# Copying the spare rows of the experts' buffer in 18 parts during the attention steps, on one Trainium2 core

## What is computed

```python
hp = layer_norm(concat([meta, x_prompt]));  hs = layer_norm(x_sample)
q_g, k_g, v_g, r_g, log_a, q_a, k_a, v_a, gate_a, gate_b = split(h @ w_in)
o_g = gated linear attention (4 heads, chunks)      # y_g = rms(o_g) * silu(r_g)
o_a = sliding-window attention (16 heads, window 128, bias, sinks)
h1  = layer_norm(ALPHA * h + (sigmoid(gate_a) * y_g + sigmoid(gate_b) * o_a) @ w_out)
f   = sum over the top 2 of 32 experts of w * (silu(x @ w_gate) * (x @ w_up)) @ w_down
h2  = layer_norm(ALPHA * h1 + f)
```

## Time and profile before

| | us |
|---|---|
| median of 3 runs | 1911.17 (1908.79 to 1911.86) |
| profiled execution, its own time | 1909.03 |
| its span, first to last instruction | 1906.9 |
| TensorE busy | 1734.5 (91%) |
| VectorE busy | 1221.0 (64%) |
| ScalarE busy | 883.9 (46%) |
| GpSimd busy | 306.3 (16%) |
| chain that ended last: TensorE's share | 40% |

### The profile page before, as it was taken

One profiled execution on the slowest core, in us unless ns is written; L12 is line 12 of the kernel. 1 busy time (PEld: TensorE's weight loads), 2 busy tenths in 40 slices (PEclk: granted clock), 3 DMA queues, 4 the chain that ended last, 5 costly groups with the idle time before them and its releaser, 6 DMA issues. The chain is left out here.

```text
span 1906.9 us, 28797 instructions
## 1 busy us (share of the span) xinstructions
PE 1734.5 (91%) x9022; PEld 1463.8 (77%) x9022; DVE 1221.0 (64%) x1695; ACT 883.9 (46%) x1446; POOL 306.3 (16%) x386
## 2 busy tenths in 40 slices
PE   4899999899899999999978899379999999999955
PEld 4889999688788878878846788268888888888832
DVE  6411110577778767777753333868988988988917
ACT  4322221344344434444411122338778778788723
POOL 3200000122412232232210111010000010010025
PEclk9889999899999999999967899579999999999978
DMA  6379521434333333422359424379999999999854
GB/s 207 108 238 289 171 68 52 142 103 144 115 123 125 126 130 103 158 90 89 95 191 321 146 99 185 123 273 397 419 411 414 417 411 409 419 413 408 330 214 194
DMA packets 183312, 422.90 MB, mean 222 GB/s; under 512 B 24976, under 2 KB 123168, under 8 KB 158424
## 3 DMA queue, kind: packets, MB, share of 16 engines
q1 hardware_dynamic: 129776, 321.93, 45.8%
q0 software_dynamic: 20048, 69.06, 10.2%
q10 hardware_dynamic: 33408, 30.94, 4.6%
HBM read 354.83 MB, written 78.55 MB: 227 GB/s over the span
## 5 line engine op out<-in xcount | busy, mean ns | idle before, releaser
L1801 DVE TENSOR_TENSOR wm_lo<-raw,wm_hi 128x2048 fp32r<-128x2048 f32 x192 | 434.3, 2290 | 70.1 <-ACT wm_hi L1297 66.5
L1297 ACT CAST wm_hi<-raw 128x2048 fp32r<-128x2048 f32 x192 | 363.4, 1912 | 72.9 <-PE PS L1934 44.8
L1932 PE MATMUL PS<-w_hi,hT_hl 128*128 128x512 f32 (+1 forms) x584 | 232.9, 399 | 12.0 <-DMA hT_hl<-hl_dram 7.1
L1933 PE MATMUL PS<-w_lo,hT_hl 128*128 128x512 f32 (+1 forms) x584 | 227.0, 389 | 0.0
L1934 PE MATMUL PS<-w_hi,hT_hl 128*128 128x512 f32 (+1 forms) x584 | 226.6, 388 | 0.0
L1932 PE MATMUL PS<-wm_hi,xT_hi 128*128 128x512 f32 x512 | 203.7, 398 | 2.9 <-DVE xT_lo L1863 2.9
L1934 PE MATMUL PS<-wm_hi,xT_lo 128*128 128x512 f32 x512 | 200.8, 392 | 0.0
L1933 PE MATMUL PS<-wm_lo,xT_hi 128*128 128x512 f32 x512 | 200.3, 391 | 0.0
L1972 PE MATMUL PS<-xa_hi,wn 128*128 128x384 f32 x480 | 162.1, 338 | 0.2 <-ACT ev L1063 0.2
L1974 PE MATMUL PS<-xa_hi,wn 128*128 128x384 f32 x480 | 161.3, 336 | 0.0
L1973 PE MATMUL PS<-xa_lo,wn 128*128 128x384 f32 x480 | 161.2, 336 | 0.0
(11 more groups left out here) (340 smaller groups left out, 3403.2 us busy)
## 6 DMA issues: line engine op xcount, KB each, us to landing
raw<-in_w_gate SPq DMA_DIRECT2D x64, 1024.0 KB, 6.7
raw<-in_w_up SPq DMA_DIRECT2D x64, 1024.0 KB, 7.5
raw<-in_w_down SPq DMA_DIRECT2D x64, 1024.0 KB, 8.4
hT_hl<-hl_dram POOLq DMA_DIRECT2D x70, 512.0 KB, 5.2
braw<-in_w_in SPq DMA_DIRECT2D x16, 1024.0 KB, 6.2
obuf_dram<-yb ACTq DMA_DIRECT2D x32, 512.0 KB, 8.2
nd_dram<-ev ACTq DMA_DIRECT2D x72, 192.0 KB, 2.1
nd<-nd_dram SPq DMA_DIRECT2D x36, 384.0 KB, 3.4
```

What stands on the lines that cost most here:

```text
L1297: act.copy(wm_hi[:, j], raw[:, j]).then_inc(m_hi[j // 4], 1)
L1801: dve.tensor_tensor(wm_lo[:, j], raw[:, j], BF(wm_hi[:, j]), ALU.subtract).then_inc(m_lo[j // 4], 1)
L1932: pe.matmul(out, x_hi, w_hi_, start=start, stop=False)
L1933: pe.matmul(out, x_hi, w_lo_, start=False, stop=False)
```

## The change

The two copies of 4,608 KB at L755 are taken out. In their place each block k of `h_dram` is copied alone to its two places in the spare blocks, 18 transfers of 512 KB, with the same semaphore. They are issued by SP in attention, two at a time, right behind `ka_load(g, b)` in the steps b = 3, 4 and 5 of the groups 0, 1 and 2. The three waits on `s_out` count 18 copies in place of 2.

```diff
+        def spare_rows(k):
+            for a in range(2):
+                sp.dma_start(obuf_dram[(NE + a * NB + k) * P:(NE + a * NB + k + 1) * P, :], h_dram[k]).then_inc(s_out, 16)
+
@@ the loop over the steps of a group on SP
                 if b > 1:
                     nd_load(g, b, s, n0 + b)
                 ka_load(g, b, s, n0 + b)
+                if g < 3 and b in (3, 4, 5):
+                    spare_rows(3 * g + b - 3)
                 if g + 1 < G and b in (1, 7):
                     wide_load(g + 1, 0 if b == 1 else 2)
@@ behind the loads for the sample tokens on SP
-        for a in range(2):
-            sp.dma_start(obuf_dram[(NE + a * NB) * P:(NE + (a + 1) * NB) * P, :],
-                         h_dram.rearrange("b p n -> (b p) n")).then_inc(s_out, 16)
         for k in range(2):
             mg_load(k, k)
@@ three waits, two on SP and one on ACT
-        sp.wait_ge(s_out, 16 * (G + 2))
+        sp.wait_ge(s_out, 16 * (G + 2 * NB))
```

More of the change, by code:

```diff
@@ L1306, in _ @@
         act.wait_ge(d_route, 1)
-        act.wait_ge(s_out, 16 * (G + 2))
+        act.wait_ge(s_out, 16 * (G + 2 * NB))
         iters = 15 + (act.value_load(novr[0:1, 0:1], min_val=0, max_val=16) + 1) // 2
```

## The result

The changed kernel takes 1931.32 us (median of 4 runs, 1926.74 to 1938.63) against 1911.51 (4 runs, 1908.79 to 1913.82) before: the ratio is 1.0106, 95% interval 1.0084 to 1.0128. It is slower by about 20 us, where 4.5 were forecast, and lies outside the range given. The profiled execution is the fastest of the four, 1926.74, so the traces explain 17.7 us: 1926.74 - 1909.03.

What follows compares the result with a forecast made beforehand. TensorE was taken as the bound, busy 1734.5 of 1906.9 us. Removal 0 plus 9 steps x 0.5 us made 4.5 us slower: 1911.2 + 4.5 = 1915.7 us, range 1909.5 to 1922 for 8 times in 10.

Steps and rivals of the forecast that it cites:

- The removal, gain 0: At the output projection: taking out the large copies gains 0, since no wait there ends with a transfer.
- A wait set free: Rival, at 1049 us: a 3.04 us wait belongs to a transfer behind the copies; up to 3.0 us back, 1908.2 us; chance 0.08.
- SP's issues and the late `nd`, 0: Attention: a pair holds SP 0.7 to 1.3 us; `nd` at worst some 0.7 us late; cost taken as 0.
- The three waits that count 18 copies, 0: Waits on `s_out`: counting 18 copies costs nothing, as all land hundreds of microseconds ahead of the first wait.
- The slack of `hT`, 0.5 us: Attention step: `hT` is complete by about 407.5 us and TensorE needs it at 408.05, about 0.5 us slack.
- The delay of `hT`: Attention: a pair delays `hT` by 0.5 to 2.9 us, a stall of 0 to 2.4; taken as 0.5 a step.
- the discount for the packets: Attention: copies' 47 KB packets start engines at once, one reason for a stall below a wide load's 0.8 us: 0.5.
- The rate of a pair: Transfer engines in attention: a pair moves 1.05 MB at 307 GB/s and takes 3.4 us of all 16 engines.
- Three steps share one stall: Attention steps with pairs: a stall delays TensorE's next start, giving the next step more slack; neighbouring steps partly share one.
- Nine steps at 0.5: Attention: nine steps with a stall of 0.5 us each, 4.5 us slower in all.
- The granted clock: TensorE in attention: clock stays at 1.00 beside the fullest wide load; no cost was counted.
- packets in the way: Rival, in attention: engines finish begun packets, so `hT` waits for the whole pair; 1.4 us stall, 11 us, 1922 us; chance 0.14.

Runs made afterwards that it cites:

- both sets of copies: Changed kernel with the two large copies put back at their old place, the 18 copies staying: 1934.51 us, ratio 1.0116.
- `hT` early: Changed kernel with POOL issuing `hT` one place earlier: 1905.63 us, 0.9959; the same edit on the kernel before: 1904.05 us, 0.9941.
- The small packets: Changed kernel with each copy cut into runs of 1 KB, same bytes: 1934.31 us, ratio 1.0095.
- the loads: Changed kernel with each pair replaced by two 512 KB loads to an unused SBUF tile, large copies back: 1923.48 us, ratio 1.004.
- Half a step later: Changed kernel with the pairs issued in steps 4 to 6, after the running step's products with the values: 1915.02 us, ratio 0.9998.
- The added transposes: Changed kernel with 15 unread transposes behind steps 2, 4 and 6 of groups 0 to 2: 1923.72 us, ratio 1.0058.
- The second run of the changed kernel: Changed kernel run again, unaltered, as base beside the 1 KB copies: 1936.21 us, ratio 1.0106.
- Pairs in steps 3 and 5 only: Changed kernel with the three pairs of step 4 moved behind attention, to the old place: 1929.28 us, ratio 1.0092.

## Why the prediction was wrong, step by step

- **The removal, gain 0:** right. The start of the output projection still follows VectorE's merge, and with both sets of copies nothing changes. "A wait set free" is out.
- **SP's issues and the late `nd`, 0:** right. A pair holds SP for 1.23 us (within the 0.7 to 1.3 given), `nd` lands in 8.0 us, and with `hT` early the copies still stand ahead of `nd`, with no wait seen.
- **The three waits that count 18 copies, 0:** right; the last copy is issued at 746.8 us.
- **The slack of `hT`, 0.5 us:** right. The slower half went from 6.3 to 8.2 us in the first of the nine steps, 1.9 us, and TensorE waited 1.16: the slack was 0.7 there.
- **The delay of `hT`, taken near the low end of 0.5 to 2.9 us, for a stall of 0.5 us a step:** this is the step that failed first. The delay was 1.5 to 2.6 us in the steps 3 and 5 (slower halves of 8.1 to 8.4 in place of 5.5 to 6.9), and the waits there 1.16 to 1.57. I had let the copies use all of the idle time of the 7 us from 401. But idle time only helps `hT` if it comes before its last packet is due; much of it lies where the transfers have been issued and nothing moves yet, or behind the landing (this is argued from the stretches; no run tests it). I had also taken a lead of 1.5 us for the copies, and it was 0.9 to 1.2. And I had made the stall smaller than a wide load's mean, 0.8, on the word of the large packets. The small packets show that their size matters little; the loads show that two times 512 KB harms even as a load, and that the copy adds to it. So the discount for the packets had no ground. The wide loads' own 0.8 a step, 7.2 us for nine, was nearer to the 8.5 measured; with loads in place of the copies the six waits came to 6.2 us. Why one wide load of 1 MB does less in some steps stays open.
- **The rate of a pair:** right. I took 307 GB/s, 3.4 us; the first pair had 328 GB/s, 3.2 us, and the pair that ran alone in "Half a step later" took 2.9 us (47.5% of the engines from 393 to 399). The 436 GB/s of the Trainium skill ("DMA: Bandwidth & Descriptors", section "Anatomy of one DMA — SWDGE (gpsimd) path") were further off. The same page of the Trainium skill, section "Latency and other measured facts", has 207 to 214 GB/s for copies between tensors in HBM, with other shapes; by that a pair takes an estimated 5 us. This trace lies between the page's two figures, close to my row; the rate was not what failed.
- **Three steps share one stall:** right, and stronger than said. The step behind a wait has none; without its pair the time is the same. Beside the slack that I had named, the late start also takes away the copies' lead over `hT`.
- **Nine steps at 0.5:** six waits with a mean of 1.4 us, 8.5 in place of 4.5 us. With this alone the time would have been 1911.2 + 8.5 = 1919.7, in the range.
- **The granted clock:** this term was missing. The prediction said that it stays at 1.00 beside the fullest wide load. It had looked at 452 to 459 us, a stretch without a wait. The longest wait in its own rows ends at 478.38, and the trace of the kernel before has, right behind it:

```profile
478.38 0.47 PE L1932 MATMUL PS<-w_hi,hT_hl 128*128 128x512 f32 x1 [1.93 <-issue]
479.15 0.40 PE L1932 MATMUL PS<-w_hi,hT_hl 128*128 128x512 f32 x1
479.85 0.60 PE L1932 MATMUL PS<-w_hi,hT_hl 128*128 128x512 f32 x1
481.11 0.63 PE L1932 MATMUL PS<-w_hi,hT_hl 128*128 128x512 f32 x1
482.38 0.63 PE L1932 MATMUL PS<-w_hi,hT_hl 128*128 128x512 f32 x1
```

So a wait was known to cost more than its length. I had put the term at nothing; it is about 6.4 of the 7.1 us of longer products in the profiled execution, and it brought the time out of the range. The Trainium skill, "TensorE: Matmul & The Clock Gate", "Part 1: The HAM clock gate (the "warmup" mystery)", has the clock halved when TensorE idles. The added transposes agree, though here not every wait brings it.

- **The rival "packets in the way"** had nearly the right wait, 1.4 us, by 3.4 - 1.5 - 0.5, and 11 us in all. Its mechanism did not hold: in 1 KB packets the copies delay `hT` as much. The working holds without packets: the pair is served first, and what is left of it when `hT` is issued is the delay: 3.2 less a lead of about 1.1 is 2.1 us, the mean of the delays in steps 3 and 5.

What the account leaves: 8.8 us idle and 7.1 us of longer products, most of it half clock, make the 15.9 of attention. The medians differ by 4 us more than that. The second run of the changed kernel had eight stretches at half clock in place of six and 46.0 us idle in place of 41.7, and was 7 us slower. So part of the spread of the changed kernel (12 us in four runs) fits the same cause, though I have only two of its profiles. The kernel before spreads as well: 5 us in its first four runs, but 14 us in the 14 runs taken beside "Pairs in steps 3 and 5 only".

## What to carry to other kernels

Before placing a transfer beside a full engine, find the next transfer that somebody waits for, and how long before its need it lands: half a step later, or half the size, was free here, and the same bytes 1 us ahead of `hT` cost 1%. Price a wait of TensorE by the rows behind it as well as by its length, since the products after it may run at half clock. And where a prefetched tile lands just in time, issue it earlier in its own queue first: this removed the harm, and made the kernel 0.4 to 0.6% faster than before.

## What was unexpected of the hardware

- Waits of 1.16 to 1.57 us were followed by some 3 to 4 us at 1.2 GHz in some steps and not in others: behind 1.57, 1.52 and 1.46 it fell, behind 1.55, 1.25 and 1.16 it didn't, and not even behind 2.19 us at 844.50.
- Two copies of 512 KB within HBM moved at 328 GB/s and landed in 5.4 us; loads of the same bytes landed in 4.4.
- 1 MB issued about 1 us ahead of another queue's load was served mostly before it, in packets of 32 KB and of 1 KB alike: in the 4 us from 384 the two queues moved 1.05 and 0.20 MB with large packets, 0.86 and 0.13 with small ones.
- Without the large copies, SP issued the state stores in 8.24 in place of 35.18 us. Most of a queue's issue time went with the transfers ahead of it here, and that was worth nothing.
